# Three pairs of down units by seven products in two of the three blocks, the residual kept in memory meanwhile, and the low half of up's second block made by a transfer that adds

## The reference, cut to what matters

```python
def swiglu(x, wg, wu, wd):
    return (jax.nn.silu(x @ wg) * (x @ wu)) @ wd
# DEPTH = 2, D_MODEL = 1024, D_FF = 2816, SEQ = 512 + DEC_BATCH = 8 tokens
x = x + 0.5 * swiglu(rms_norm(x, n_ffn1[i]), w_ffn1_gate[i], w_ffn1_up[i], w_ffn1_down[i])
...            # a mixer: gated chunks and a linear recurrence, then an output matmul
x = x + 0.5 * swiglu(rms_norm(x, n_ffn2[i]), w_ffn2_gate[i], w_ffn2_up[i], w_ffn2_down[i])
...            # a gate by one more matmul and a small projection; at the very end a norm
```

## Time and profile before

| | |
|---|---|
| median of 3 runs | 1888.15 us (1887.84 to 1888.51) |
| the profiled execution, its time | 1887.87 us |
| its span | 1885.7 us |
| PE busy | 1850.9 us (98%), 15112 matmuls |
| DVE, ACT, POOL busy | 1371.3, 946.9, 215.7 us |
| transfers | 233.42 MB, 124 GB/s on average |

### The profile page before, as it was taken

One profiled execution on the slowest core, in us unless ns is written; L12 is line 12 of the kernel. 1 busy time (PEld: TensorE's weight loads), 2 busy tenths in 40 slices (PEclk: granted clock), 3 DMA queues, 4 the chain that ended last, 5 costly groups with the idle time before them and its releaser, 6 DMA issues.

```text
span 1885.7 us, 37225 instructions
## 1 busy us (share of the span) xinstructions
PE 1850.9 (98%) x15112; PEld 1831.2 (97%) x15112; DVE 1371.3 (73%) x2041; ACT 946.9 (50%) x1363; POOL 215.7 (11%) x261
## 2 busy tenths in 40 slices
PE   6999999999999999999999999999999999999996
PEld 6999999998999999999999999999999999999996
DVE  7867848768688577587687587577785875866775
ACT  6635526446456255365465264454544653634553
POOL 0000000340110000002110000013202000000012
PEclk9999999999999999999999999999999999999998
DMA  5635546522345464454345364463222545635541
GB/s 159 157 108 147 144 106 155 161 79 68 91 104 153 113 151 129 118 151 144 101 105 145 101 163 128 125 169 112 68 90 90 135 124 131 151 115 134 144 136 46
DMA packets 65724, 233.42 MB, mean 124 GB/s; under 512 B 7376, under 2 KB 9712, under 8 KB 65568
## 3 DMA queue, kind: packets, MB, share of 16 engines
q1 hardware_dynamic: 52576, 184.87, 30.6%
q0 software_dynamic: 12992, 46.32, 14.8%
HBM read 228.86 MB, written 2.31 MB: 123 GB/s over the span
## 4 chain that ended last, share of the span: by engine, by line
PE 96%; DVE 2%; ACT 1%; DMA 1%; issue 0%; DVEq 0%; SPq 0%; ACTq 0%
PE main L773 21%; PE main L633 20%; PE main L599 18%; PE main L638 10%; PE aux L633 8%; PE aux L773 6%; PE aux L638 4%; PE aux L863 2%; PE main L678 2%; PE aux L599 1%; PE aux L811 1%; PE main L863 1%; PE aux L883 0%; DVE rstd_b L1356 0%; DMA w_lo<-weights_dram 0%
## 5 line engine op out<-in xcount | busy, mean ns | idle before, releaser
L959 ACT ACTIVATE w_hi<-raw 128x1024 fp32r<-128x1024 f32 (+1 forms) x184 | 187.4, 1030 | 118.5 <-PE main L773 66.0
L633 PE MATMUL main<-part_hi,w_hi 128*128 128x260 f32 x960 | 240.8, 283 | 3.7 <-DVE tmp L1495 3.7
L633 PE MATMUL main<-part_lo,w_hi 128*128 128x260 f32 x960 | 240.8, 283 | 0.0
L1344 DVE TENSOR_TENSOR w_lo<-raw,w_hi 128x1024 fp32r<-128x1024 f32 (+1 forms) x184 | 221.9, 1207 | 23.2 <-ACT w_hi L959 22.1
L773 PE MATMUL main<-part_hi,w_lo 128*128 128x260 f32 x1080 | 217.5, 283 | 0.0
L773 PE MATMUL main<-part_hi,w_hi 128*128 128x260 f32 x1080 | 217.1, 282 | 0.0
L773 PE MATMUL main<-part_lo,w_hi 128*128 128x260 f32 x1080 | 216.9, 282 | 0.0
L553 POOL DMA_DIRECT2D w_lo<-weights_dram x80 | 68.8, 860 | 1126.5 <-ACT w_lo L989 1126.5
L599 PE MATMUL main<-part_hi,w_hi 128*128 128x260 f32 x944 | 192.6, 285 | 2.0 <-DVE tmp L1489 2.0
L599 PE MATMUL main<-part_hi,w_lo 128*128 128x260 f32 x944 | 189.8, 283 | 0.0
L599 PE MATMUL main<-part_lo,w_hi 128*128 128x260 f32 x944 | 189.4, 282 | 0.0
(11 more groups left out here) (250 smaller groups left out, 3982.0 us busy)
## 6 DMA issues: line engine op xcount, KB each, us to landing
raw<-weights_dram SPq DMA_DIRECT2D x344, 512.0 KB, 3.7
w_lo<-weights_dram POOLq DMA_DIRECT2D x80, 512.0 KB, 6.5
x<-x_in_dram SPq DMA_DIRECT2D x4, 520.0 KB, 6.9
y_out<-x SPq DMA_DIRECT2D x8, 260.0 KB, 2.6
mix<-p_in_dram POOLq DMA_DIRECT2D x2, 520.0 KB, 4.0
tau<-ln_dram POOLq DMA_DIRECT2D x2, 512.0 KB, 3.8
tau<-ws_dram POOLq DMA_DIRECT2D x2, 512.0 KB, 6.1
bs<-bs_dram POOLq DMA_DIRECT2D x2, 256.0 KB, 4.0
```

The lines of the kernel that those rows point to most:

```text
L633: pe.matmul(ps, hi_w[:, w], xx(k), start=(start and k == 0 and b == 0), stop=False, skip_group_check=True)
L959: act.activation(w_hi[:, s, 0:c], raw[:, s, 0:c], ACT.Copy).then_inc(whi, 1)
L1344: dve.tensor_tensor(w_lo[:, s, 0:c], raw[:, s, 0:c], w_hi[:, s, 0:c], ALU.subtract).then_inc(wlo, 1)
```

## The change

**Down by pairs.** In the first two blocks of each FFN only the down units 0 and 1 are still done plainly, right behind the block's tiles. The units 2 to 7 become three pairs, each done by the seven products as tiles 0, 1 and 2 of the block that follows (so the blocks have 6, 11 and 9 such tiles). Their x side is not `sig` but sums of the hidden tiles, two tiles at a time: `sums_raw` (three DVE instructions), `sums_hi` (ACT), `sums_lo` (DVE), four times a block. The third block does its 8 down units plainly, as before.

**Where x goes.** The sums take the place of `x` in SBUF (raw sums and low parts in the same bytes; the high parts in `parts`, `sum2`, `sum3`). So `x` is written to memory (`x_spill`) while the squares are summed, and the down results of the first two blocks are scaled by 0.5 times the norm and sent to memory, 16 transfers of 260 KB an FFN (`d_part`). In the third block, once its three pairs are done, POOL loads `x` back and then issues two transfers that add `d_part[0]` and `d_part[1]` to it, each after the one before has landed. DVE's evacuation of the last down units waits for them. The two plain hidden tiles are copied into `x`'s place by a transfer (`copy_lead`), which the first `c22` of the FFN waits for.

**Up's second block.** `hi_b` gets a second ACT instruction, the negative into `wx_part(.., 1)`, and POOL issues a transfer that adds the up unit's half (`up_low`, 256 KB). DVE's `lo_b` shrinks to a copy of one element that counts `wlo`. P3 waits for the transfer ahead of its last four matmuls.

**Beside these.** `softplus`, 25 tiny DVE instructions of the first layer, is cut in three and moved into the second block of the first FFN; the tile buffers go by a running number; `bd` shares its place with `sum3` and is cleared by POOL once a layer.

The core of the diff:

```diff
+DOWN_PAIRS = KH - 1
+DOWN_CHUNKS = sum(t == XT for t in FFN_CHUNKS)
+def tiles_of(c):
+    return down_pairs(c) + FFN_CHUNKS[c] - (0 if c else LEAD)
...
+            def up_low(n, T_):
+                pool.wait_ge(up_neg, T_ + 1)
+                pool.dma_start(wx_part(T_, 1), weights[n + 1, :, HB:2 * HB],
+                               accum_op=ALU.add).then_inc(up_lo[T_ % 2], 16)
+            def copy_lead(f, G):
+                pool.wait_ge(evac, G)
+                pool.wait_ge(sx_raw, 4 * KH * (f + 1))
...
+                pool.dma_start(x[:, XT - 2:XT, :], tmp[:, 2:4, :]).then_inc(lead_copy, 16)
...
             def gates(l, which):
...
+                    for t in range(tiles_of(c)):
+                        gate_low(n + 2 * t, S + t)
+                        if t:
+                            up_low(n + 2 * t - 2, S + t - 1)
+                        if c == 0 and t == 1:
+                            copy_lead(f, G)
...
+                        if c and DOWN_PAIRS <= t < 2 * DOWN_PAIRS:
+                            second_out(t - DOWN_PAIRS)
+                        if c and 2 <= t < 2 + DOWN_PAIRS:
+                            first_out(t - 2)
+                        if c == DOWN_CHUNKS and t == 5:
+                            pool.wait_ge(unit, n + 2 * DOWN_PAIRS)
+                            pool.dma_start(x[:, :, :], x_spill if f else x_in).then_inc(reload_s, 16)
+                        if c == DOWN_CHUNKS and t == 6:
+                            for b in range(4):
+                                pool.wait_ge(d_out[b], 16 * sent_by(f, b))
+                            pool.wait_ge(reload_s, 48 * f + 16)
+                            pool.dma_start(x[:, :, :], d_part[0], accum_op=ALU.add,
+                                           max_dma_last_dim=8 * TOK).then_inc(reload_s, 16)
+                        if c == DOWN_CHUNKS and t == 7:
+                            pool.wait_ge(reload_s, 48 * f + 32)
+                            pool.dma_start(x[:, :, :], d_part[1], accum_op=ALU.add,
+                                           max_dma_last_dim=8 * TOK).then_inc(reload_s, 16)
+                    up_low(n + 2 * t, S + t)
...
-                        product(Z(G, t), wx_part(t, 0), wx_part(t, 1), *s4, False, True,
-                                low=(wlo, n + 2 * t + 2)).then_inc(unit, 2)
+                        product(Z(G, S + t), wx_part(S + t, 0), wx_part(S + t, 1),
+                                *(hidden_sum(c - 1, 4) if down(t) else s4), False, True,
+                                low=(up_lo[(S + t) % 2], 16 * ((S + t) // 2 + 1))).then_inc(unit, 2)
...
+            def sums_hi(l, f, c, i):
+                act.wait_ge(sh_raw, 3 * sums_of(f, c, i))
+                act.activation(sum_hi(l, i), sum_raw(i), ACT.Copy).then_inc(sh_hi, 1)
...
-                act.activation(wx_part(t, 0), raw_up(n, 1), ACT.Copy).then_inc(hib_s, 1)
+                act.activation(wx_part(T_, 1), raw_up(n, 1), ACT.Copy, scale=-1.0).then_inc(up_neg, 1)
+                act.activation(wx_part(T_, 0), raw_up(n, 1), ACT.Copy).then_inc(hib_s, 1)
...
+                dve.tensor_tensor(to[:, 0:2, :], v[:, 0:4:3, :] if c == 0 else v[:, 1:3, :],
+                                  v[:, a + 1:a + 2, :].broadcast_to([P, 2, HALF]), ALU.subtract).then_inc(sh_raw, 1)
+                dve.wait_ge(sh_raw, at + 1)
+                dve.scalar_tensor_tensor(to[:, 2, :], v[:, a, :], -1.0, to[:, SUM_AT[c][1], :],
+                                         ALU.mult, ALU.subtract).then_inc(sh_raw, 1)
+                dve.wait_ge(sh_raw, at + 2)
+                dve.scalar_tensor_tensor(to[:, 3, :], v[:, b, :], -1.0, to[:, 2, :],
+                                         ALU.mult, ALU.subtract).then_inc(sh_raw, 1)
+            def sums_lo(l, f, c, i):
+                dve.wait_ge(sh_hi, sums_of(f, c, i))
+                dve.tensor_tensor(sum_lo(i), sum_raw(i), sum_hi(l, i), ALU.subtract).then_inc(sh_lo, 1)
...
-                dve.tensor_tensor(wx_part(t, 1), raw_up(n, 1), wx_part(t, 0), ALU.subtract).then_inc(wlo, 1)
+                dve.tensor_copy(small[:, 60:61], eps).then_inc(wlo, 1)
...
+                        if not last and t >= pairs and k % 2:
+                            dve.wait_ge(hf_s, products_of(l, h) + t - pairs + 1)
+                            sums_raw(f, c, k // 2)
+                        if first and t == 2:
+                            sums_raw(f, c, 0)
...
                     for g in range(1, tiles - 1):
                         tau_sums(g + 1, (tau3, tau4))
                         c12(g - 1)
                         hidden(g - 1)
+                        tile_sums(g - 1)
                         c22(g)
                         lo12(n + 2 * g + 2, S + g + 1)
-                        lo_b(n + 2 * g + 2, S + g + 1, g + 1)
+                        lo_b(n + 2 * g + 2, S + g + 1)
...
+                        tile_sums_lo(g - 1)
...
+                        dve.wait_ge(reload_s, 48 * (f + 1))
```

More of the change, by code:

```diff
@@ L266, in trunk @@
         hib_s = sem("hib_s")
+        up_neg = sem("up_neg")
+        up_lo = [sem(f"up_lo{b}") for b in range(2)]
         prod = sem("prod")
+        sh_raw = sem("sh_raw")
+        sh_hi = sem("sh_hi")
+        sh_lo = sem("sh_lo")
+        lead_copy = sem("lead_copy")
+        d_second = sem("d_second")
+        d_out = [sem(f"d_out{b}") for b in range(4)]
+        spilled = sem("spilled")
+        reload_s = sem("reload_s")
+        bd_zero = sem("bd_zero")
         p1_copy = sem("p1_copy")
@@ L1055, in ffn @@
                 n, G, h = l * UNITS + u0, l * GROUPS + g0, l * HT + which * (HT0 + XT)
-                S = first_tile(l, which)
+                S, f = first_tile(l, which), 2 * l + which
                 for c, whole in enumerate(FFN_CHUNKS):
-                    first = c == 0
-                    tiles = whole
+                    first, last = c == 0, c == DOWN_CHUNKS
+                    pairs, tiles = down_pairs(c), tiles_of(c)
                     if first:
@@ L1179, in ffn @@
                             hi12(n + 2 * g + 4, S + g + 2)
+                        if f == 0 and c == 1 and g == 1:
+                            act.wait_ge(lamv, 1)
+                            act.activation(lt[:, 1, :], lt[:, 0, :], ACT.Exp).then_inc(lama, 1)
                     t = tiles - 1
-                    gate(t + 2)
-                    h_hi(t - 1)
-                    silu(t)
-                    h_hi(t)
-                    done(t, "P4")
-                    hi(d + 2, 2, False)
-                    for j in range(XT):
-                        if c == 2:
+                    if not last:
+                        down_hi(d, 3)
+                        h_hi(t - 1)
+                        gate_cut(d + 2, S + tiles)
+                        done(t, "P4")
+                        down_hi(d + 1, 2)
+                        silu(t)
+                        h_hi(t)
+                        gate_cut(d + 4, S + tiles + 1)
+                        hidden_sums(t)
+                        n, G, h, S = d + 2, D + 2, h + tiles - pairs, S + tiles
+                    else:
+                        gate(t + 2)
+                        h_hi(t - 1)
+                        silu(t)
+                        h_hi(t)
+                        done(t, "P4")
+                        hi(d + 2, 2, False)
+                        for j in range(XT):
                             hi(d + j + AHEAD, (j + AHEAD) % SLOTS)
@@ L1368, in split_lo, with softplus @@
                                   ALU.subtract).then_inc(hlo, 1)
-            def softplus():
-                step = [0]
+            def softplus(part):
+                step = [(0, 1, 12)[part]]
                 def lam(ins):
@@ new lines, in tile_sums_lo, with down_out @@
+                    def tile_sums_lo(t):
+                        k = whole - tiles + t
+                        if not last and t >= pairs and k % 2:
+                            sums_lo(l, f, c, k // 2)
+                        if first and t == 2:
+                            sums_lo(l, f, c, 0)
+                    def down_out(j):
+                        dve.wait_ge(unit, d + j + 1)
+                        free(2 + j)
+                        dve.scalar_tensor_tensor(halves(T(2 + j)), pair(down_bank(G, which, c, j)), 0.5,
+                                                 halves(rstd_b[:, :]), ALU.mult, ALU.mult).then_inc(evac, 1)
+                        to_send(2 + j)
@@ L1623, in ffn @@
                     lo34(n + 2, S + 1)
+                    if f == 0 and c == 1:
+                        softplus(0)
                     tau_sums(2, (tau1, tau2))
@@ L1918, in ffn @@
             for o in range(XT):
-                put(columns(down, o, f, tiles))
+                block = columns(down, o, f, tiles)
+                if tiles == XT:
+                    block = block.reshape(P, KH, 2, P).transpose(0, 2, 1, 3).reshape(P, XT * P)
+                put(block)
             f += tiles
```

519 lines of the change are left out of this document (341 added, 178 removed).

## The result

The changed kernel takes 1935.75 us (median of 4 runs, 1935.44 to 1938.63), the one before 1888.33 us on the same chip (1887.84 to 1888.66). The ratio is 1.0255, 95% interval 1.0237 to 1.0273: slower by 2.5%. The forecast was 1942, its range 1856 to 1970.

The account below looks back on a forecast made before the run. It took PE's chain as the bound, with big transfers in POOL's queue delaying the gate: 1887.9 - 34.6 (matmuls) + 7.2 (DVE) + 70.4 (gate waits) + 11.5 (slow clock) = 1942.4, taken as 1942 us, range 1856 to 1970.

Parts of the forecast that it names:

- The first step: Whole kernel: PE is 96% of the chain, so 288 fewer matmuls at 0.120 us take off 34.6 us.
- The first rival: POOL's queue, third block: the gate's 512 KB pass beside a big transfer, nothing held up; 1860.5 us, chance 0.24.
- reload landed: Third block: x's plain reload, queued behind gate 5, up 4 and a send, lands 7.8 us after cycle 4 starts.
- wait for gate 6: Third block: the gate's transfer for tile 6, queued behind the reload, comes 0.6 us after PE needs it.
- wait for gate 7: Third block: the gate's transfer for tile 7, queued behind the first adding transfer, makes PE wait 8.5 us.
- from gate 7 to gate 8: Third block: up 6, the second adding transfer and the gate in series, 18.6 us, of which PE covers 10.08.
- wait for gate 8: Third block: the gate's transfer for tile 8, behind the second adding transfer, makes PE wait 8.5 us again.
- late `c22`: First block: sums in successive cycles make DVE late, P4 0.9 us late in two cycles an FFN, 7.2 us in all.
- waits for the gate: Third blocks: PE waits for gate transfers held up in POOL's queue, 17.6 us an FFN, 70.4 over four.
- the 1.2 GHz level: PE's slow clock behind an idle stretch: 1.44 us lost for each of eight waits, 11.5 us.
- They hold up little: Third block: in order, but adding at 223 GB/s throughout without sharing, 4.8 us an FFN; 1879.7, up to 1900; chance 0.14.
- They hold up more: Third block: adding at 156 GB/s throughout, 3.2 us more each, 25.6 in all, 1968 us; chance 0.12.

Follow-up runs that it names:

- 1: Changed kernel with both big adding transfers cut to 8 elements a partition, queue positions and waits kept, x then incomplete: 1876.43 us, ratio 0.9935.
- 5: Changed kernel with x coming back in quarters of 520 KB, each with its own counter and wait, most behind the last up transfer: 1878.40 us, ratio 0.9951.
- 3: Changed kernel with both big adding transfers issued whole behind the last gate transfer of the block, all data moved: 1920.83 us, ratio 1.0175.
- 4: Kernel before with only the second part added (ACT's negation, 80 adding transfers of 256 KB, DVE's one-element copy), no pairs: 1888.26 us, ratio 1.0001.
- 6: Changed kernel without its second part: DVE's subtraction back, no up transfers in POOL's queue, big transfers whole: 1916.50 us, ratio 1.0148.
- 7: Changed kernel with x back in quarters and without the second part (DVE's subtraction back, no up transfers): 1862.78 us, ratio 0.9864.
- 9: Quarters kernel, up transfers kept, without POOL's wait for the last quarter ahead of the next layer's parameter loads: 1867.94 us, ratio 0.9892.
- experiment 2: Changed kernel with both big adding transfers made plain, overwriting x, same bytes and positions, packets of 16640 instead of 4160 bytes: 1888.90 us, ratio 1.0001.

## Why the prediction was right, and where its sizes were off

**The first step holds.** 15112 matmuls became 14824, at 0.120 us. The first rival's outcome appears where the big transfers are empty (1, 1876.43) or cut and moved (5, 1878.40; without the second part of the change 1862.78, 2.3 above that rival's 1860.5). Its premise, that a queue lets 512 KB pass a big one, is refuted by gate 7, which landed 3 us behind the first adding transfer, 18.9 us after its issue. That the loss comes from the adding transfers' bytes is shown by taking only those away (1), and that they hold the gates up by standing ahead of them by moving them (3). That this alone is not enough, and that cutting them, with a wait of DVE for each quarter, gives the rest, is shown by 5 against 3. How much of a wait is the order in POOL's queue and how much the 16 engines being full (busy for 0.95 of the third block) stays open: no run has the gate's transfer in another queue, where it would meet full engines too; SP's units of 512 KB, in theirs, landed in 8.3 us there (median of seven), 3.7 before.

**The steps of the third block.** In the first FFN, the start of cycle 4 by the forecast's reckoning is 293.1 (P1's need, 304.16, less 11.04).

| step | forecast | measured |
|---|---|---|
| reload landed | T4+7.8 | T4+8.6 |
| wait for gate 6 | 0.6 | 1.27 |
| from gate 6 to gate 7 | 18.6 | 19.0 |
| wait for gate 7 | 8.5 | 8.62 |
| from gate 7 to gate 8 | 18.6 | 15.4 |
| PE's work in that | 10.08 | 12.44 |
| wait for gate 8 | 8.5 | 2.94 |

Up to gate 7 the queue's reckoning came out within some 1 us (the first adding transfer landed 1.7 us later than forecast, at T4+28.1, and the gate closer behind it). The step that failed is the one from gate 7 to gate 8. I let the second adding transfer begin where gate 7 and up 6 had passed, in strict series. In fact it was issued at 322.12, 2.3 us ahead of PE's start on gate 7; from the landing of the first adding transfer (321.2) to gate 8 (339.76) it took 18.6 us, where I had 22.4. Then the slow clock stretched PE's cycle by 2.1 us against the one before it, and so covered part of the wait that was left. Over four FFNs the waits of gate 7 are 31.4 us (34 forecast), of gate 8 13.0 (34), of gate 6 5.1 (2.4).

**The sum, term by term.**

| term | forecast | measured | from |
|---|---|---|---|
| matmuls | -34.6 | -34.6 | count, by 0.120 |
| late `c22` | +7.2 | +7.3 | PE's waits for L1847 |
| waits for the gate | +70.4 | +48.2 | 50.4 less the 2.2 of before |
| the 1.2 GHz level | +11.5 | +18.6 | PE's work at a granted 0.50: 47.6 us, 10.4 before, half of each |
| PE busy beyond that | nothing | +6.8 | PE busy 1841.7, less 1850.9 - 34.6, less 18.6 |
| sum | +54.5 | +46.3 | span: +48.2 |

The 1.9 us left over are not accounted for; the waits put down to "issue" at L762 (5.5 us, 3.6 before) are as long. The 6.8 us fit the first matmuls behind a wait: the cycle behind gate 6 took 10.33 us at full clock in place of 10.08, and PE has 31 waits in place of 8, which at 0.25 each makes 5.8, an estimate. The waits are 22 us less than forecast, the clock 7 us more, and the last 6.8 no term had, so most of the errors cancel: that 1942 came so close is partly chance.

**The clock.** I priced the slow level from one row of before, 1.44 us behind a gap of 2.5, the same for each of eight waits. A longer wait costs more: 0.50 was granted from 318.90 to 329.10, ahead of gate 7's landing and for 4.7 us of PE's work behind it. Not all time at half clock is lost, only PE's work in it: in the four third blocks the trace has nine stretches at 0.50, 51.2 us together, in which PE worked 35.6, so 17.8 us are lost there, where eight times 1.44 are 11.5. Of experiment 1, too, the waits are only a part: between the two profiled executions, 57.1 us apart, lie 44.0 of waits for the gate (50.4 less 6.4) and 15.4 of PE's busy time (1841.7 less 1826.3), less 2.4 more for `c22`.

**DVE.** Its total was right, by the wrong parts. The two late cycles are there, and cost less. PE's timeline:

```profile
89.97 0.39 PE L762 MATMUL main<-part_hi,w_hi 128*128 128x260 f32 x1 [0.59 <-DVE tmp L1847]
...
101.04 0.39 PE L762 MATMUL main<-part_hi,w_hi 128*128 128x260 f32 x1 [0.71 <-DVE tmp L1847]
```

and DVE's in the first of them, the three sums in a row, then `c22` without a wait of its own, where it waited 1.10 us before:

```profile
87.95 0.69 DVE L1609 TENSOR_TENSOR x<-x 128x520 f32<-128x520 f32 x1
...
89.14 0.43 DVE L1615 SCALAR_TENSOR_TENSOR x<-x 128x260 f32<-128x260 f32 x1
89.49 0.42 DVE L1847 TENSOR_TENSOR tmp<-main,mix 128x260 f32<-128x260 f32 x1
```

They make 4 x 1.30 = 5.2 us. The other 2.1 are what I had at nothing: 1.24 us behind `copy_lead`, whose landing took 7.3 us there (T+3.7 and 7.3 is past T+8.7, its need), and two of 0.46 and 0.36 in the second block of the first FFN (at 163.9 and 174.6), the first behind the landing of a send. Behind `softplus` and ACT's part the rows show no other wait of PE, and the later cycles of that block run at 10.08, as forecast.

**Up's transfers** cost nothing alone (4). The forecast counted them at nothing in an ordinary cycle and at 1.7 us ahead of each gate of the third block. Together with the pairs they cost 19.3 us with whole transfers (6), most of it there: 12.4 of waits for the gate and 7.0 of PE's busy time. With quarters they cost 15.6 (7), and that the forecast didn't have: they delay `copy_lead`, the sends and the last quarter, and each of those had a waiter that it named as covered or not at all, `c22` and POOL's own parameter loads (10.5 of the 15.6, by 9).

**The other rivals.** "They hold up little" asks for a cheaper transfer; the plain ones of experiment 2 are that case, 11.8 us and 1888.9, and the adding ones are not. "They hold up more" had the size of the transfers nearly right (16.6, against a forecast of 13.1 and an edge of 16.3 with the raw units), but not the time, since the steps overlapped. DVE as the bound is refuted: from 175 to 215 it is busy 37.5 of 40 us, and PE has no gap.

**Slips in the forecast's rows.** The 13 slices of the adding transfer run from 60 to 223 GB/s, not from 75; their average is as stated. A raw unit at 381 GB/s takes 1.4 us, not 1.3. The second adds under 2 us to the sum.

The Trainium skill, DMA: Bandwidth & Descriptors, section Anatomy of one DMA, gives about 2.0 us and the bytes over 436 GB/s, an estimate of 6.9 us for 2.13 MB. Beside the other traffic of these blocks the trace shows 11.8 for the plain and 16.6 for the adding one, and the measurement decides.

## What to carry to other kernels

A queue is a resource of its own: list, with their sizes, everything that shares it with the transfer PE waits for, and ask how long the pieces ahead of it hold it up. Here moving the adding transfers whole behind the last gate took 15 us off, and cutting them into quarters as well, with a wait for each, 57 (1935.75 to 1878.40). A part that costs nothing alone has to be priced again in the fuller queue, and every waiter on a transfer named, those on the queue's own engine too; and a wait of PE has to be priced with the slow clock and the restart behind it, which here came to half as much again (25.4 us on 48.2).

## What the runs showed of the hardware

An adding transfer of 2.13 MB took 16.6 us to land where a plain one took 11.8, in the same place (experiment 2), and its packets held the engines twice as long: 0.33 us for 4160 bytes, 0.16 for plain ones of that size. The half clock set in during a wait of 8.62 us, 3.1 us after PE's last matmul, and was granted for 10.2 us; 4.7 us of that fell on work, so that the next cycle took 12.44 us for 84 matmuls and hid some of the next wait. Adding 256 KB a tile to a queue with room changed nothing, and in the queue with the pairs it took the median landing of a 260 KB send from 5.0 to 7.6 us, and of SP's own weight units, in another queue, from 3.7 to 4.7.
